# Key and value transposes, gates, products and the meta chain of a gated DeltaNet moved into the last groups of the input projection, its row matrices given to GpSimd, and filler matmuls added

## The reference, cut to what matters

```python
for l in range(DEPTH):
    u = rms_norm(h, attn_norm_w[l])
    (dn_q, dn_k, dn_v, dn_z, dn_b, dn_a, df_q, ...) = split_columns(u @ w_in[l])
    y_dn = gated_deltanet(...); y_df = diff_attention(...); y_ml = mla_attention(...)
    h = h + concatenate([y_dn, y_df, y_ml]) @ w_out[l]
    h = h + (swiglu(...) if l % 2 == 0 else moe_swiglu(...))

# gated_deltanet, in each direction, on chunks, 4 heads of 128:
q, k = l2_normalize(silu(conv(q))), l2_normalize(silu(conv(k)));  v = silu(conv(v))
beta = sigmoid(b);  g = -exp(a_log) * softplus(a + dt_bias);  gc = cumsum(g)
decay = exp(gc_i - gc_j) on the lower triangle
a_mat = strict((k * beta) @ k.T * decay);  qk = q @ k.T * decay
value, k_cumdecay = (I + a_mat)^-1 @ (v * beta), (I + a_mat)^-1 @ (k * beta * exp(gc))
# then per chunk: v_new = value - k_cumdecay @ S; out = (q e^gc) @ S + qk @ v_new; S updated
```

## Time and profile before

| what | value |
|---|---|
| median of 3 runs | 1974.53 us (1974.48 to 1975.61) |
| the profiled execution's own time | 1975.23 us |
| its span, first to last instruction | 1973.4 us |
| busy, share of the span | PE 96%, DVE 75%, ACT 57%, POOL 6% |
| mean granted clock of TensorE | 0.979 of full speed |
| GpSimd's and SP's part in the mixers | 107 instructions on POOL; 440.66 MB read from HBM |

### The profile page before, as it was taken

How to read it: one execution, slowest core, us unless ns; L and a number is a source line. 1 busy time by engine, 2 the same in 40 slices (tenths; PEclk the granted TensorE clock), 3 DMA queues, 4 the chain that set the end, 5 groups by cost and what they waited for, 6 DMA issues and landing times.

```text
span 1973.4 us, 27118 instructions
## 1 busy us (share of the span) xinstructions
PE 1902.5 (96%) x10976; PEld 1626.6 (82%) x10976; DVE 1480.8 (75%) x1828; ACT 1125.5 (57%) x1249; POOL 117.7 (6%) x107
## 2 busy tenths in 40 slices
PE   9998989899999979999999999999999999999998
PEld 8987768899998967779888888888888888888886
DVE  8659666655549566756688888989889788888986
ACT  5644424433334633424677777677777777777775
POOL 1004131000000004140000000000000000000000
PEclk9998989999999998999899999999999999999999
DMA  7500001544453200005599999989999899999994
GB/s 298 177 28 1 1 1 68 200 171 171 155 182 134 97 28 1 1 3 180 191 364 345 353 352 366 352 333 353 358 360 347 340 358 351 358 356 364 356 361 178
DMA packets 64195, 443.56 MB, mean 225 GB/s; under 512 B 8172, under 2 KB 8204, under 8 KB 13632
## 3 DMA queue, kind: packets, MB, share of 16 engines
q1 hardware_dynamic: 62032, 437.87, 59.2%
q0 software_dynamic: 1760, 3.78, 0.5%
q10 hardware_dynamic: 272, 0.10, 0.0%
HBM read 440.66 MB, written 2.17 MB: 224 GB/s over the span
## 4 chain that ended last, share of the span: by engine, by line
PE 88%; DVE 10%; issue 2%; ACT 0%; DMA 0%; POOL 0%; SPq 0%; DVEq 0%; POOLq 0%; ACTq 0%
PE ps L1916 23%; PE ps L1918 23%; PE ps L1917 23%; PE ps L2311 2%; PE ps L2296 2%; PE ps L2315 2%; PE ps L1929 2%; DVE w_lo L1186 2%; DVE cacc L1278 2%; PE ps L2490 1%; PE ps L2090 1%; PE ps L2501 1%; PE ps L2137 1%; PE ps L2173 1%; PE ps L2102 0%
## 5 line engine op out<-in xcount | busy, mean ns | idle before, releaser
L1243 DVE TENSOR_TENSOR m_lo<-raw,m_hi 128x2048 fp32r<-128x2048 f32 x336 | 768.3, 2289 | 135.9 <-ACT m_hi L839 135.7
L839 ACT ACTIVATE m_hi<-raw 128x2048 fp32r<-128x2048 f32 x336 | 644.1, 1918 | 269.1 <-PE ps L1918 269.0
L1916 PE MATMUL ps<-m_hi,xe_hi 128*128 128x512 f32 x896 | 358.6, 400 | 0.0
L1918 PE MATMUL ps<-m_lo,xe_hi 128*128 128x512 f32 x896 | 353.6, 395 | 0.0
L1917 PE MATMUL ps<-m_hi,xe_lo 128*128 128x512 f32 x896 | 353.6, 395 | 0.0
L1186 DVE TENSOR_TENSOR w_lo<-raw,w_hi 128x1024 fp32r<-128x1024 f32 (+1 forms) x164 | 183.2, 1155 | 116.3 <-ACT w_hi L804 116.3
L1916 PE MATMUL ps<-u_hi,w_hi 128*128 128x272 f32 x800 | 236.7, 296 | 14.3 <-DVE u_lo L1236 9.9
L1918 PE MATMUL ps<-u_lo,w_hi 128*128 128x272 f32 x800 | 232.9, 291 | 0.0
L1917 PE MATMUL ps<-u_hi,w_lo 128*128 128x272 f32 x800 | 231.9, 290 | 0.0
L804 ACT ACTIVATE w_hi<-raw 128x1024 fp32r<-128x1024 f32 (+1 forms) x164 | 159.5, 1002 | 116.5 <-PE ps L1918 107.5
L1918 PEld LDWEIGHTS ps<-m_lo,xe_hi 128*128 128x128 f32 x896 | 168.0, 187 | 41.1
(11 more groups left out here) (397 smaller groups left out, 2765.4 us busy)
## 6 DMA issues: line engine op xcount, KB each, us to landing
raw<-in_moe_units SPq DMA_DIRECT2D x336, 1024.0 KB, 4.8
raw<-in_dense_units SPq DMA_DIRECT2D x57, 1024.0 KB, 4.8
raw<-in_dense_units SPq DMA_DIRECT2D x16, 768.0 KB, 5.6
raw<-in_dense_units SPq DMA_DIRECT2D x8, 896.0 KB, 4.5
w_uq<-in_mla_w_uq SPq DMA_DIRECT2D x2, 768.0 KB, 4.6
mats<-in_c_mats POOLq DMA_DIRECT2D x1, 1216.0 KB, 10.5
h<-in_h_rows SPq DMA_DIRECT2D x2, 544.0 KB, 4.4
bias_rows<-bias_row POOLq DMA_DIRECT2D x1, 1088.0 KB, 25.9
```

The source lines that it names most:

```text
L839: nc.scalar.activation(m_hi[k % RING][:, :], raw[:, slot, :], ACT.Copy).then_inc(m_hi_ready, 1)
L1243: V.tensor_tensor(m_lo[k % RING][:, :], raw[:, mslot(k), :], m_hi[k % RING][:, :].bitcast(F32), ALU.subtract).then_inc(m_lo_ready, 1)
L1916: mm(o, w[0], x[0], start=first, stop=False)
L1918: return mm(o, w[0], x[1], start=False, stop=last)
```

## The change

The DeltaNet's front moves into groups j = 10 to 15, as `delta_parts(j)` on PE, ACT and DVE. On PE it stands behind the stream of group j, on DVE behind the scale factors of group j, on ACT ahead of the copy of group j out of PSUM. `m_tok`, `m_rows` are steps of the meta chain. After group 15 only q·k of tile 1 is left. The row matrices are made by GpSimd in buffers of their own (`row_parts`), those of s = 1 right behind those of s = 0. The four token matrices `k_tok`, `v_tok`, `kk`, `qk` now lie in slots 4 and 5 of `raw`, so the first two units of the out-projection wait for their last readers, and the latent attention's weights `w_uq`, `w_ukv` are issued ahead of these units. GpSimd no longer makes the side product `kw` for s = 1, which had no reader. Turns of the other mixers are placed differently for s = 0: one fewer ahead of the products L1603, one more ahead of step `ks` behind the levels; their total is the same. Fillers (`idle_products`) are added at six places: behind the last product, at s = 1 ahead of level 0, ahead of the latent attention's first scores, and in layer 0 ahead of the gate and up projections (20), ahead of the down projection (8) and behind it (11). The diff is cut to these; ACT's part (the copies of `k_tok` and `v_tok`, the exponentials of the gates and of the meta chain) is moved in the same way.

```diff
@@ DVE @@
+                def delta_parts(j):
+                    if j == 10:
+                        dve.wait_ge(evac["act"], groups[plan[l]["in"][9]][2])
...
+                    if j == 11:
+                        act_w("e_alog")
...
+                        V.reciprocal(beta_t[:, :], e_beta[:, :])
+                    if j == 12:
+                        act_w("softplus")
...
+                    if j == 13:
+                        pe_w("gate_cols")
...
+                        pe_w("m_tok")
+                        S.mark(V.tensor_copy(mt[:, :, :], heads(ps[:, PAIR[1], :])), "m_tok")
+                        V.tensor_scalar(X["T"], mat(M_TRIM), g_m, None, ALU.mult)
+                        S.mark(V.tensor_scalar(X["TT"], ident, b_m, None, ALU.mult), "m_rows")
+                    if j == 14:
+                        pe_w("m_rows")
...
+                        product("kk", kk, 0, PAIR[1])
+                    if j == 15:
+                        product("qk", qk, 0, PAIR[1])
+                        act_w("m_expcols")
...
                 for i in range(NORM_JOBS - 2, NORM_JOBS):
                     mixer_scale(i)
+                product("kk", kk, 1, PAIR[1])
+                product("qk", qk, 1, 3)
@@ DVE, between the levels of s = 0 and s = 1 @@
-                    if s == 0:
-                        for d in range(2):
-                            pe_w("vnew", s, d)
-                            block_rows(1, d)
@@ PE @@
+                def delta_parts(j):
+                    if j == 10:
+                        pe.wait_ge(conv_act, 6 * (l + 1))
+                        tokens_of("v_tok", 8)
+                    if j == 11:
+                        pe.wait_ge(rstd_used, factors_before + 2 * H)
+                        act_w("v_tok", 1)
+                        tokens_of("k_tok", 4)
+                    if j == 12:
+                        dve_w("gates")
+                        act_w("k_tok", 0)
...
+                    if j == 13:
+                        dve_w("m_rows")
...
+                        product("kk", 4, 0, PAIR[1])
+                    if j == 14:
+                        dve_w("kk", 0)
+                        product("qk", 0, 0, PAIR[1])
+                    if j == 15:
+                        dve_w("qk", 0)
+                        product("kk", 4, 1, PAIR[1])
...
                 pe.wait_ge(evac["act"], groups[plan[l]["in"][-1]][2])
+                product("qk", 0, 1, 3)
+                idle_products(5, 0)
                 pe.wait_ge(rstd_used, norms_before)
...
+                                if s and d == 0:
+                                    act_w("expcols", s, d)
+                                    idle_products(10, 0)
...
+                                pe.wait_ge(log_taken, stat[0])
+                                idle_products(9, 4)
                                 dve_ml.wait(pe, 0, "qrot", H - 1)
...
+                    idle_products(20)
...
+                    idle_products(8)
                     pe.wait_ge(hid_ready, 11)
                     residual(plan[l]["down"], (hid_hi, hid_lo), cs, T)
+                    idle_products(11)
@@ GpSimd @@
+                dn_dve.wait(pool, l, "gate_cols")
+                for s in range(2):
+                    if s:
+                        dn_pe.wait(pool, l, "rows", 0, 1)
+                    for d in range(2):
+                        t = (s, 1 - s)[d]
+                        rg, rb = row_parts[s][d]
+                        nc.gpsimd.tensor_tensor(rg[:, :, :], bc(mat(M_TRI + d), 1, H), bc(gcol[:, t, 0, 4 * d:4 * d + 4], 2, P), ALU.mult)
+                        dn_pool.mark(nc.gpsimd.tensor_tensor(rb[:, :, :], bc(ident, 1, H), bc(gcol[:, t, 1, 4 * d:4 * d + 4], 2, P), ALU.mult),
+                                     "rows", s, d)
@@ SP @@
+                        dn_pool.wait(sp, l, "vb", 1, 1)
+                    if u == out_units[l][1]:
+                        dn_pool.wait(sp, l, "pt_tri", 1, 1)
```

More of the change, by code:

```diff
@@ L295, in dn_orders @@
             pe += [("state", s, d) for d in range(2)]
-            dve += [("rows", 1, d) for d in range(2)]
         dve += [("out", s, d) for d in range(2)]
@@ L310, in dn_pool_order @@
 def dn_pool_order():
-    out = []
+    out = [("rows", s, d) for s in range(2) for d in range(2)]
     for s in range(2):
@@ L465, in program @@
         qk = put("qk", [P, 2, H, P])
+        assert mark[0] == raw_at + 6 * UNIT * 4
+        put, mark = region(u_at)
+        row_parts = [[nc.alloc_sbuf_tensor_at(f"dn_r{x}0{d}", [P, H, P], F32, offset=o + d * H * P * 4) for x, o in
+                      (("g", o_dn_at), ("b", state_at))] for d in range(2)], [[put(f"dn_r{x}1{d}", [P, H, P]) for x in "gb"] for d in range(2)]
         put, mark = region(split_at)
@@ L1322, in mixer_scale, with product @@
                         weighted([(dk[:, i - 14, :], C_DK)])()
+                S = dn_dve
+                S.begin(l)
+                act_w = lambda *x: dn_act.wait(dve, l, *x)
+                pe_w = lambda *x: dn_pe.wait(dve, l, *x)
+                own = lambda *x: S.wait(dve, l, *x)
+                X = {k: v[:, :] for k, v in mm_t.items()}
+                g_m, b_m = cols[:, 42:43], cols[:, 43:44]
+                def product(x, dst, t, bank):
+                    pe_w(x, t)
+                    S.mark(V.tensor_copy(dst[:, t, :, :], heads(ps[:, bank, :])), x, t)
@@ L1489, in _ @@
                 turn_of_others = lambda: next(others, None)
-                S = dn_dve
-                S.begin(l)
-                act_w = lambda *x: dn_act.wait(dve, l, *x)
-                pe_w = lambda *x: dn_pe.wait(dve, l, *x)
-                own = lambda *x: S.wait(dve, l, *x)
-                def products(t):
-                    for x, dst, b in (("kk", kk, 2), ("qk", qk, 3)):
-                        pe_w(x, t)
-                        S.mark(V.tensor_copy(dst[:, t, :, :], heads(ps[:, b, :])), x, t)
@@ L2038, in mixer_sums, with tokens_of @@
                         sums([P], M_ONE if i < 10 else M_B64)
+                S = dn_pe
+                S.begin(l)
+                act_w = lambda *x: dn_act.wait(pe, l, *x)
+                dve_w = lambda *x: dn_dve.wait(pe, l, *x)
+                tp = nc.tensor.transpose
+                X = {k: v[:, :] for k, v in mm_t.items()}
+                factors_before = stat[0]
+                def tokens_of(x, base):
+                    for t in range(2):
+                        for hh in range(H):
+                            i = tp(ps[:, PAIR[t], P * hh:P * hh + P], qkv[:, base + hh, META + P * t:META + P * t + P], ident)
+                        S.mark(i, x, t)
@@ L2203, in _ @@
-                dve_w("gates")
-                act_w("k_tok", 1)
-                for t in range(2):
-                    for k, x in enumerate((a_t, beta_t)):
-                        c = 16 * t + 8 * k
-                        tp(ps[:, 0, c:c + 8], x[:, META + P * t:META + P * t + P], ident[0:8, 0:8])
-                for k, x in enumerate((a_t, beta_t)):
-                    i = mm(ps[:, 0, 32 + 16 * k:48 + 16 * k], small[0:8, 33:33 + P], x[:, 0:META], start=True, stop=True)
-                S.mark(i, "gate_cols")
@@ L2212, in _ @@
-                dve_w("meta_kqv")
-                act_w("v_tok", 1)
-                fk = [mt_kqv[:, x, :, :].rearrange("p r n -> p (r n)") for x in range(3)]
-                tp(ps[:, 1, 0:P], fk[0], ident)
-                tp(ps[:, 1, P:2 * P], fk[2], ident)
-                mm(ps[:, 1, 2 * P:3 * P], fk[0], fk[0], start=True, stop=True)
-                S.mark(mm(ps[:, 1, 3 * P:4 * P], fk[0], fk[1], start=True, stop=True), "m_tok")
-                turn_of_others()
-                dve_w("m_rows")
@@ L2221, in _ @@
-                X = {k: v[:, :] for k, v in mm_t.items()}
-                mm(ps[:, 3, 0:P], ones, X["T"], start=True, stop=True)
-                mm(ps[:, 3, P:2 * P], ones, X["TT"], start=True, stop=True)
-                mm(ps[:, 3, 256:257], mat(M_TRIM), cols[:, 42:43], start=True, stop=True)
-                S.mark(mm(ps[:, 3, 257:258], mat(M_B16), cols[:, 42:43], start=True, stop=True), "m_rows")
+                dve_w("m_prod")
+                dve_w("kk", 1)
+                turn_of_others()
@@ L2263, in _ @@
                     for d in range(2):
-                        dve_w("rows", s, d)
+                        dn_pool.wait(pe, l, "rows", s, d)
                         if s:
@@ L2275, in _ @@
                         if d and s == 0:
[L2276 to L2277 removed]
+                            dve_w("qk", 1)
+                        S.mark(mm(ps[:, 2 * d + 1, :], ones, flat(row_parts[s][d][1]), start=True, stop=True), "beta", s, d)
                     turn_of_others()
+                    if s == 0:
+                        turn_of_others()
                     for n in range(LEVELS):
```

233 lines of the change are left out of this document (113 added, 120 removed).

## The result

| | before | after |
|---|---|---|
| median, us (runs) | 1974.72 (1974.48 to 1975.61, 4) | 1957.97 (1957.35 to 1961.43, 4) |
| ratio to before | | 0.9893, 95% interval [0.9853, 0.9933] |
| profiled execution, its span | 1975.23, 1973.4 | 1958.37, 1956.6 |
| mean granted clock | 0.979 | 0.988 |

The change takes 16.8 us off the median, 0.8%; the ratio of the runs says 1.1%, with an interval from 0.7 to 1.5%. The forecast was 1961 us, so 3 us too slow, in its range of 1953 to 1971.

The account below looks back on a forecast made before the run. PE was taken to bound the kernel, with DVE busier in the seams. Seam 24.8, moved work -15.4, turn -0.6, GpSimd -2.0 and fillers 6.7 made 13.5 us faster: 1961 us, range 1953 to 1971.

Parts of the forecast that it names:

- What bounds: Whole kernel: PE is 88% of the chain, so stages gain only where PE waits or runs at the lower clock.
- signs named in advance: Profile after: no idle ahead of moved matmuls, products 12.2 us after last factor, weightings near 0.50; wrong if past 17.
- rival 3: Seam chain does not shorten, products 19 us after the last factor; only fillers stay, about 1974 us; chance 0.07.
- Moved work, 7.7 us a layer: In-projection: PE has no gap there, so moved matmuls lengthen it by 7.7 us a layer, 15.4 us lost.
- rival 4: In-projection: twelve waits stop PE; over 1.1 us each the gain is gone, at 1.6 the time is 1980; chance 0.08.
- The seam, 24.8: Last scale factor to first product: shrinks to 12.2 us, gaining 13.2 and 11.6 us in the two layers.
- rival 1: Seam: 1.2 GHz begins earlier, already in row and beta matrices; 7 us less gain, about 1968 us; chance 0.15.
- The turn, -0.6: Attention turn put off: 1.9 us a layer gained behind the products, 2.2 paid ahead of `ks`; net 0.6 lost.
- GpSimd, -2.0: Row matrices on GpSimd: slow DVE's softmaxes beside them in the seam; 2.0 us lost, of 6.4 at most.
- Rival 2: Seam: GpSimd's lock on DVE at its upper bound costs 4.4 us more than taken, 1966 us; chance 0.08.
- Fillers, 6.7: Idle products keep PE's clock up: gate and up 2.0, down 1.5, latent scores 1.5, s = 1 2.0 and -0.3.

Follow-up runs that it names:

- second trace: The changed kernel run once more without any edit, on another chip: 1958.29 us, ratio 0.9901.
- rows on VectorE: Changed kernel with row matrices on VectorE in their new buffers, those of s = 1 behind the two turns: 1959.8 us; placed ahead of the turns: 1967.24 us.
- seam fillers: Changed kernel with 11 instead of 5 fillers behind the last product, and 5, 6 and 8 more for s = 0: 1956.48 us; run again: 1963.52 us.
- two tests: Changed kernel without any added fillers: 1963.59 us; kernel before with the fillers alone, at five of the six places: 1969.9 us.

## Why the prediction was right, point by point

**What bounds.** Right in the main: the chain that ended last is PE for 89%. Elsewhere than in the seams, DVE sets the pace in the levels' first 16 us, and PE was not the bound in the low stretches at s = 1 of layer 0 and among the rope steps of layer 1. Of the signs named in advance, PE had no idle time ahead of the moved matmuls, the weightings in the seam took 0.50 us, the products came at 13.9 and 14.0 and not past 17 (so rival 3, with its 19, is out too), and the levels' stretch at 1.2 GHz is 13.6 us in each layer, before and after.

**Moved work, 7.7 us a layer.** The timeline of PE at the last four sums, kernel before, then changed kernel:

```profile
127.03 1.08 PE L1929 MATMUL ps<-sq,mats 128*128 128x272 f32 x4
```

```profile
133.91 1.08 PE L1949 MATMUL ps<-sq,mats 128*128 128x272 f32 x4
```

They start 6.9 us later. In layer 1 the stage is 5.5 longer, but 1.4 of low clock at its start had gone; without fillers it is 6.9 again. From the start of each moved piece to the start of the next stream matmul it is 1.7 us for the transposes (forecast 1.9), 2.7 for the three products (2.9) and 2.4 for gates and meta chain (2.6), which leaves nothing for the six changes between matmuls (0.3). The term was 0.8 a layer too large, and the stretch from the last sums to the last factor is 0.3 shorter besides: 13.2 us lost in all instead of 15.4. No stall: rival 4 is out.

**The seam, 24.8.** Measured 11.5 and 9.8, together 21.3. Where the clock stayed up (second trace, rows on VectorE, seam fillers) it is 12.2 and 12.3 long, within 0.1 of the forecast's 12.2, so 24.7 gained. Its pieces stand in the chain that ended last, changed kernel, layer 0:

```profile
136.99 0.68 DVE kk L1356
137.68 0.60 DVE qk L1356
...
139.37 1.70 PE ps L2315 x2
...
141.72 1.70 PE ps L2315 x2
...
147.94 1.01 ACT ss L996 x4
148.97 0.17 DVE cols L1507
```

Two copies 1.3, row matrices, and then the first tile's exponentials on ACT, for which DVE waits: late next was ACT, as foreseen. Only the row matrices, with the small column matmuls behind them, are off: a row matrix pair takes 1.70 where a full clock gives 1.1. So rival 1's first piece did happen, in three of the four seams of the two traces, at 1.7 to 1.9 us each. That is the missing 3.5. The prediction had argued that the low clock needs a gap of a few us; here PE had stood for 1.5 us at most. Rival 1 did not turn the sum round, because the long stretch in the levels costs nothing where DVE bounds. That these seams came out near the forecast at all rests on the five fillers, without which they were 15.5 and 15.2.

**The turn, -0.6.** The step that was mis-sized most. Behind the product the first level's result came after 6.0 us instead of 7.4 in layer 0 (157.01 - 151.00, against 163.33 - 155.95), 1.4 of the 1.9 gained. The timeline of DVE, changed kernel:

```profile
157.01 0.68 DVE L1645 TENSOR_TENSOR dn_TT<-mats,dn_M 128x512 f32<-128x512 f32 x1
```

But the turn ahead of `ks` costs more than 2.2: the levels pay 1.5 net in layer 0 and 3.7 in layer 1, 5.2 instead of 0.6. The gain in the seam, 4.5, was in the other term, so that putting the turn off loses 0.7 as a whole.

**GpSimd, -2.0.** Mis-sized: 0. GpSimd made the rows of s = 1 from 143.8 to 147.9, beside DVE's columns and differences, which read PSUM and kept their pace, and was done before the first weighting at 149.63 (0.50 us). Rival 2 is out. The old work on DVE at s = 1 was hidden, as I had said: with the rows there again the stage is 94.2 too.

**Fillers, 6.7.** The two tests give 5.6 and 5.6 by their medians, one of them across chips. By stages, before against after, with the forecast in brackets: gate and up 1.8 (2.0), down 1.5 (1.5), s = 1 of layer 0 0.7 (2.0; the fillers' own part is 0.2, by the kernel without them), of layer 1 -0.6 (-0.3), the first latent scores nothing (1.5): there PE fell to 1.2 GHz at 812, four us ahead of the fillers at 816.3, among rope steps that wait on DVE. Behind down 1.4 (nothing): the step that failed is "layer 1's first groups are bound by DVE", since with a full clock DVE fed PE 26 matmuls in 3.4 us there, without fillers 16 in 3.5. Sum 4.8 by the stages.

**What no term foresaw.** Layer 1's levels got 3.2 shorter. Before, PE ran at half speed from 752.4 to 764.6, busy all of it. After, the low stretch came earlier, over work on which DVE sets the pace. The two windows:

```profile
723.60:737.20 13.60, 11.02 (x46) 8.64 (x47) 13.07 (x33) 3.70 (x13) 5.26 (x5) 0.51 0.01 2
741.00:748.00 7.00, 7.00 (x61) 6.46 (x61) 6.49 (x23) 2.15 (x7) 1.86 (x2) 1.00 0.00 0
```

At half speed that stretch had cost 6.1 us of 12.2, an estimate. The two traces with seam fillers give 7.0 for a stretch of the same length at the same place (109.0 against 102.0). Less the turn's 3.7 that is 2.4 to 3.3, and 3.2 were measured. And the stretch ahead of the experts got 2.0 shorter in this execution, with a low clock of 3.5 us instead of 10.2. In the other traces of kernels with the same program there it was 55.1 to 56.4, so a part of the 2.0 is chance.

**The sum.** Moved work -13.2, seams +21.3, levels with the turn and GpSimd -1.5 + 3.2, fillers +4.8, experts' start +2.0: 16.6 of 16.8 us. The forecast had -15.4, +24.8, -2.6, +6.7 and nothing: 13.5. That it came so close is in part luck: its errors of 2.2, -3.5, 4.3, -1.9 and 2.0 partly cancel, and the largest of them is mostly clock that fell elsewhere.

What stays open is why the clock falls in one execution and not in the next at the same gaps, and which single gap brings a stretch: the runs fill gaps in groups and don't take them apart.

## What to carry to other kernels

Work moved off a serial seam costs its full PE time where it lands if PE has no gap there (6.9 us a layer here), so move only what the seam waits for: of three products moved here, two were not worth it, and taking them back out gave the lowest median, of four runs. Before covering a gap to keep PE's clock up, look at which engine bounds the 15 us behind it: a low clock under a DVE-bound stretch was free here, and with that stretch filled the clock fell in some executions where PE was the bound (6.5 us). Judge changes under 1% by stages between named rows of the traces, and keep executions whose clock fell elsewhere apart.

## What the runs showed of the hardware

The same program, with the same gap (1.49 and 1.48 us) ahead of the same matmuls, ran the next four us at 1.2 GHz in one execution and at 2.4 GHz in another. Single executions of one kernel spread over 4 to 21 us; between the two traces of the kernel with seam fillers, 13.4 of 14.0 us lie in the two stages in which PE's clock fell. GpSimd's multiplication of two broadcast operands, 128x512, took 1.04 us, against 1.27 for its mask of the same shape. A VectorE operation of 0.28 us on SBUF operands beside it took up to 1.08.
